# Feed-forward gate and up: the tokens' high and low parts in one 512-column matmul, with the halves added on VectorE

## The reference, cut to what matters

```python
def swiglu(u, w_in, w_out):
    a, b = jnp.split(u @ w_in, 2, axis=-1)
    return (jax.nn.silu(a) * b) @ w_out

h = h + 0.5 * swiglu(rms_norm(h, ffn1_norm), ffn1_w_in, ffn1_w_out)
...
h = h + 0.5 * swiglu(rms_norm(h, ffn2_norm), ffn2_w_in, ffn2_w_out)
```

## Time and profile before

| | before |
|---|---|
| median of 3 runs | 1435.93 us |
| profiled execution, its own time | 1435.79 us |
| its span, first to last instruction | 1434.0 us |
| PE busy | 94% of the span, 9038 matmuls |
| VectorE busy | 65% |
| ScalarE busy | 53% |
| GpSimd busy | 14% |
| mean granted TensorE clock | 0.969 |
| DMA | 263.43 MB, mean 184 GB/s |

### The profile page before, as it was taken

One profiled execution on the slowest core, in us unless ns is written; L12 is line 12 of the kernel. 1 busy time (PEld: TensorE's weight loads), 2 busy tenths in 40 slices (PEclk: granted clock), 3 DMA queues, 4 the chain that ended last, 5 costly groups with the idle time before them and its releaser, 6 DMA issues.

```text
span 1434.0 us, 22961 instructions
## 1 busy us (share of the span) xinstructions
PE 1341.9 (94%) x9038; PEld 1223.3 (85%) x9038; DVE 933.8 (65%) x1331; ACT 755.3 (53%) x1108; POOL 197.5 (14%) x163
## 2 busy tenths in 40 slices
PE   5999999979898999998989897989999999999998
PEld 5999989979698999988979787889999877787776
DVE  4655554474575555565379674584664799999996
ACT  4334345545634333355445676333653577778774
POOL 0211120021001111120020331230000000202020
PEclk9999999999999999999989899998999899999999
DMA  7666554533153665644634333324555399999991
GB/s 246 211 189 188 179 162 151 176 118 118 37 162 116 205 188 181 190 148 131 187 90 141 96 118 119 89 59 123 172 176 181 122 365 367 367 367 338 369 342 64
DMA packets 222165, 263.43 MB, mean 184 GB/s; under 512 B 14018, under 2 KB 204799, under 8 KB 221951
## 3 DMA queue, kind: packets, MB, share of 16 engines
q1 hardware_dynamic: 219520, 260.39, 56.8%
q10 hardware_dynamic: 2558, 1.86, 0.4%
HBM read 261.17 MB, written 1.05 MB: 183 GB/s over the span
## 4 chain that ended last, share of the span: by engine, by line
PE 75%; DVE 14%; ACT 6%; issue 2%; POOL 1%; DMA 1%; ACTq 0%; DVEq 0%; POOLq 0%
PE bank L526 23%; PE bank L528 22%; PE bank L527 22%; DVE sb_wlo L483 3%; DVE sb_wlo L470 3%; PE bank L621 1%; DVE sb_XC L1880 1%; PE bank L2502 1%; ACT sb_whi L464 1%; ACT sb_aw L1546 1%; DMA sb_pos<-in_positions 1%; DVE sb_st L1120 1%; PE bank L2565 1%; PE bank L2537 0%; ACT sb_sgh L1115 0%
## 5 line engine op out<-in xcount | busy, mean ns | idle before, releaser
L470 DVE TENSOR_TENSOR sb_wlo<-sb_raw,sb_whi 128x1024 fp32r<-128x1024 f32 (+4 forms) x306 | 389.4, 1316 | 224.3 <-ACT sb_whi L464 224.2
L464 ACT ACTIVATE sb_whi<-sb_raw 128x1024 fp32r<-128x1024 f32 (+4 forms) x306 | 301.4, 1037 | 238.4 <-PE bank L528 238.2
L526 PE MATMUL bank<-sb_Uh,sb_whi 128*128 128x256 f32 x1216 | 348.9, 287 | 9.2 <-DVE sb_wlo L470 5.2
L527 PE MATMUL bank<-sb_Ul,sb_whi 128*128 128x256 f32 x1216 | 346.6, 285 | 0.0
L528 PE MATMUL bank<-sb_Uh,sb_wlo 128*128 128x256 f32 x1216 | 346.4, 285 | 0.0
L526 PEld LDWEIGHTS bank<-sb_Uh,sb_whi 128*128 128x128 f32 x1216 | 236.0, 194 | 13.1 <-issue 10.1
L527 PEld LDWEIGHTS bank<-sb_Ul,sb_whi 128*128 128x128 f32 x1216 | 236.1, 194 | 0.8
L528 PEld LDWEIGHTS bank<-sb_Uh,sb_wlo 128*128 128x128 f32 x1216 | 235.9, 194 | 0.0
L526 PE MATMUL bank<-sb_whi,sb_Uh 128*128 128x256 f32 (+3 forms) x560 | 159.5, 285 | 1.1 <-DVE sb_Ul L611 0.7
L527 PE MATMUL bank<-sb_wlo,sb_Uh 128*128 128x256 f32 (+3 forms) x560 | 159.2, 284 | 0.0
L528 PE MATMUL bank<-sb_whi,sb_Ul 128*128 128x256 f32 (+3 forms) x560 | 159.1, 284 | 0.0
(11 more groups left out here) (408 smaller groups left out, 2250.3 us busy)
## 6 DMA issues: line engine op xcount, KB each, us to landing
sb_raw<-in_w_in SPq DMA_DIRECT2D x104, 512.0 KB, 4.4
sb_raw<-in_ffn_w_in SPq DMA_DIRECT2D x88, 512.0 KB, 4.5
sb_raw<-in_ffn_w_out SPq DMA_DIRECT2D x44, 512.0 KB, 3.7
sb_raw<-in_w_down SPq DMA_DIRECT2D x26, 512.0 KB, 6.9
sb_raw<-in_w_gate SPq DMA_DIRECT2D x25, 512.0 KB, 6.8
sb_raw<-in_w_up SPq DMA_DIRECT2D x25, 512.0 KB, 7.2
sb_raw<-in_w_out SPq DMA_DIRECT2D x16, 512.0 KB, 4.5
sb_raw<-in_w_ssd_branch SPq DMA_DIRECT2D x16, 512.0 KB, 4.4
```

The costliest lines, as they stand in the source:

```text
L464: nc.scalar.activation(whi[:, i % NSLOT, c], raw[:, i % NSLOT, c], ACT.Copy).then_inc(S("hi_done"), 1)
L470: nc.vector.tensor_tensor(wlo[:, i % NSLOT, c], raw[:, i % NSLOT, c], whi[:, i % NSLOT, c].bitcast(F32), ALU.subtract).then_inc(S("lo_done ...
L526: pe.matmul(o, lh, rh, start=start, stop=False, skip_group_check=True)
L527: pe.matmul(o, lh, rl, start=False, stop=False, skip_group_check=True)
```

## The change

Gate and up get two banks each, 4 and 5, 6 and 7, one per block n of 128 features. `Uh` and `Ul` become the two halves of one tensor `U`, so that for a chunk k the high and the low part of the 256 tokens can be one moving operand of two runs of 256 columns, 2048 elements (8 KB) apart. `by_feature_wide` does each triple in two matmuls: high weights with both parts, 512 columns, and low weights with the high part, 256 columns into the first half of the bank. So the first half of a bank holds high × high + low × high, the second half high × low. VectorE adds the halves of two banks in one reduction over a pair (512 sums of two). Gate's sum goes to `sgh[:, 0]`, where SiLU is taken in place, up's sum to `sgh[:, 1]`, where the product is made in place. The semaphore `ffn_sum` counts the sums; the PE's next gate or up waits for it instead of `_silu` or `_mul`. At its start `pe_ffn` claims banks 4 to 7 instead of 4 and 5. VectorE's order in the loop is: up's sum and product of chunk i, low splits of U(i+1) and D(i), gate's sum of chunk i + 1, low split of G(i+2).

```diff
-        bank = [ctx.enter_context(nc.psum_tensor(f"bank{i}", [P, 512], F32)) for i in range(8)]
+        bank = [ctx.enter_context(nc.psum_tensor(f"bank{i}", [P, 512], F32)) for i in range(4)]
+        wide_banks = ctx.enter_context(nc.psum_tensor("wide_banks", [P, 4, 512], F32))
+        bank += [wide_banks[:, i] for i in range(4)]
...
-            Uh = sb("Uh", [P, KD, T], F32R, pa)
-            Ul = sb("Ul", [P, KD, T], F32R, pa)
+            U = sb("U", [P, 2, KD, T], F32R, pa)
+        Uh, Ul = U[:, 0], U[:, 1]
...
+        def by_feature_wide(i, b):
+            wh, wl = wslab(i, KD, 256)
+            for n in range(2):
+                f, o = slice(n * P, (n + 1) * P), bank[b + n]
+                arriving = fresh.pop() if fresh else None
+                for k in range(KD):
+                    if arriving is not None:
+                        pe.wait_ge(*reach(arriving[0], k + 1))
+                    pe.matmul(o.rearrange("p (a n) -> p a n", a=2), wh[:, k, f], U[:, :, k], start=k == 0, stop=False, skip_group_check=True)
+                    last = pe.matmul(o[:, 0:T], wl[:, k, f], Uh[:, k], start=False, stop=k == KD - 1, skip_group_check=True)
+            return last
...
-            claim(4, nm + "_silu", n)
-            claim(5, nm + "_mul", n)
+            for j in range(4):
+                claim(4 + j, nm + "_sum", 2 * n - 1 + j // 2)
...
-                for j, done in enumerate(("_silu", "_mul")):
+                for j in range(2):
                     pe.wait_ge(*reach("lo_done", 2 * (g + j + 1 + off)))
                     if i is not None:
-                        pe.wait_ge(*reach(nm + done, i))
-                    by_feature(g + j, 4 + j, Uh, Ul, KD, 256).then_inc(S("slab_used"), 1)
+                        pe.wait_ge(*reach(nm + "_sum", 2 * i - 1 + j))
+                    by_feature_wide(g + j, 4 + 2 * j).then_inc(S("slab_used"), 1)
...
-            def silu(i, used_by):
-                act.wait_ge(*reach("slab_used", used_by))
-                if not (isinstance(i, int) and i == 0):
-                    act.wait_ge(*reach(nm + "_mul", i))
-                act.activation(sgh[:, 0], bank[4][:, :], ACT.Silu).then_inc(S(nm + "_silu"), 1)
+            def silu(i):
+                act.wait_ge(*reach(nm + "_sum", 2 * i + 1))
+                act.activation(sgh[:, 0], sgh[:, 0], ACT.Silu).then_inc(S(nm + "_silu"), 1)
...
+            halves_of = [wide_banks[:, 2 * j:2 * j + 2].rearrange("p c (a n) -> p c n a", a=2) for j in range(2)]
+
+            def gate_sum(i, used_by):
+                dve.wait_ge(*reach("slab_used", used_by))
+                if not (isinstance(i, int) and i == 0):
+                    dve.wait_ge(*reach(nm + "_mul", i))
+                dve.tensor_reduce(sgh[:, 0].rearrange("p (c n) -> p c n", c=2), halves_of[0], AX, ALU.add).then_inc(S(nm + "_sum"), 1)
+
             def mul(i, used_by):
                 dve.wait_ge(*reach("slab_used", used_by))
-                dve.wait_ge(*reach(nm + "_silu", i + 1))
                 if not (isinstance(i, int) and i == 0):
                     dve.wait_ge(*reach(nm + "_h", i))
-                dve.tensor_tensor(sgh[:, 1], sgh[:, 0], bank[5][:, :], ALU.mult).then_inc(S(nm + "_mul"), 1)
+                dve.tensor_reduce(sgh[:, 1].rearrange("p (c n) -> p c n", c=2), halves_of[1], AX, ALU.add).then_inc(S(nm + "_sum"), 1)
+                dve.wait_ge(*reach(nm + "_sum", 2 * i + 2))
+                dve.wait_ge(*reach(nm + "_silu", i + 1))
+                dve.tensor_tensor(sgh[:, 1], sgh[:, 0], sgh[:, 1], ALU.mult).then_inc(S(nm + "_mul"), 1)

             lo_upto(nm)
+            gate_sum(0, b + 1)
             mul(0, b + 2)
-            for k in range(3):
-                split_lo(b + 3 + k)
+            split_lo(b + 3)
+            split_lo(b + 4)
+            gate_sum(1, b + 3)
+            split_lo(b + 5)
             with dve.Fori(1, n - 1) as i:
                 mul(i, i * 3 + b + 1)
-                for k in range(3):
-                    split_lo(b + 3 + k, i)
+                split_lo(b + 3, i)
+                split_lo(b + 4, i)
+                gate_sum(i + 1, i * 3 + b + 3)
+                split_lo(b + 5, i)
```

More of the change, by code:

```diff
@@ L115, in two_blocks @@
                   [("ffn_" + k, [(nm + "_" + k, n) for nm, n in ffns]) for k in ("silu", "mul", "h", "hh")],
+                  [("ffn_sum", [("ffn1_sum", 2 * NF), ("ffn2_sum", 2 * NF)])],
                   [("ffn_x", [("ffn1_x", 4), ("ffn2_x", 4)]), ("ffn_acc", [("ffn1_acc", 3), ("ffn2_acc", 3)])],
@@ L669, in act_ffn @@
             b = slab_of[nm]
-            def silu(i, used_by):
-                act.wait_ge(*reach("slab_used", used_by))
-                if not (isinstance(i, int) and i == 0):
-                    act.wait_ge(*reach(nm + "_mul", i))
-                act.activation(sgh[:, 0], bank[4][:, :], ACT.Silu).then_inc(S(nm + "_silu"), 1)
+            def silu(i):
+                act.wait_ge(*reach(nm + "_sum", 2 * i + 1))
+                act.activation(sgh[:, 0], sgh[:, 0], ACT.Silu).then_inc(S(nm + "_silu"), 1)
             hi_upto(nm)
-            silu(0, b + 1)
+            silu(0)
             for k in range(3):
@@ L681, in act_ffn @@
             with act.Fori(1, n - 1) as i:
-                silu(i, i * 3 + b)
+                silu(i)
                 for k in range(3):
@@ L685, in act_ffn @@
             nxt["hi"] = b + 3 * n
-            silu(n - 1, b + 3 * (n - 1))
+            silu(n - 1)
             hi_upto(b + 3 * n - 1)
```

## The result

The changed kernel takes 1438.7 us (median of 20 runs, 1437.32 to 1444.07), the kernel before 1436.28 us over 20 runs beside them: the ratio is 1.0017, with a 95% interval of 1.0009 to 1.0025. It is slower by 0.17%, less than the 0.5% that the prediction called distinguishable, but the interval lies wholly above 1. The prediction had 1435.3 us, a gain of 0.6 us. The time lies inside its range; the direction was wrong.

A forecast was written before the change was run, and what follows sets the result against it. It took TensorE, busy throughout both feed-forward loops, as the bound. Matmul saving and edges, −5.4 + 0.4 + 1.6 + 0.1 + 2.7 = −0.6 us on a profiled 1435.79, gave 1435.3 us by the median; range 1430.0 to 1442.0.

The forecast's parts named there:

- the saving of the matmuls: Gate and up: a pair at 0.352 us replaces a triple at 0.360, 672 times; 5.4 us saved, between 8.9 and 0.
- edge 2: ffn2's first matmul: claiming banks 4 to 7 makes it wait for the norm's eighth low part, +1.6 us.
- Edge 1: ffn1's first slabs: gate's sum must run after the rope angles before chunk 1's gate slab starts, +0.4 us.
- Edge 3: Chunk 1's up slab in either FFN: its low part queues behind chunk 0's sum and product; +0.1 us in ffn2, 0 in ffn1.
- Edge 4: Last hidden chunk of either FFN: VectorE's split goes first and GpSimd's operation stretches, +1.36 us, twice: 2.7 us.
- a second run of the moving operand: Wide matmul: its second run of 256 columns adds some 0.005 us to 0.227, read from the experts' gate and up.
- VectorE, ScalarE and DMA in the loop: Steady loop: VectorE's two added reductions, the later SiLU and DMA slots are covered by about 11 us, costing nothing.
- Rival A: Gate and up matmuls: the fixed part goes with the runs of columns, so nothing is saved; 1440.6 us, chance 0.13.
- Its variant by the skill's 2.5 ns: Gate and up matmuls: only 2.5 ns fixed each, so 1.7 us saved; an estimated 1438.9 us, no separate chance.
- B: Gate and up: the pitch shrinks with the mix, a pair taking 0.340 us; 1427.2 us, chance 0.07.
- C: Every wide matmul: a second run 8 KB away costs far more than the experts' 4 KB; 1449.5 us, chance 0.06.
- D: Wide matmul is split again on its way, pitch as before; same time as Rival A, within its chance of 0.13.

The follow-up runs named there:

- experiment 3: The changed kernel with the token parts interleaved by chunk, so the 512 moving columns are one contiguous run: 1438.23 us, ratio 1.0009.
- experiment 6: The changed kernel with each block's eight wide matmuls first, then its eight narrow ones: 1436.28 us, ratio 0.9995.
- experiment 1: The changed kernel with each of banks 4 to 7 claimed just ahead of its first matmul: 1435.08 us, ratio 0.9989.
- experiment 2: The kernel before with the four-bank claim alone, banks 6 and 7 also claimed at each feed-forward network's start: 1442.03 us, ratio 1.0032.
- experiment 7: The changed kernel with the last chunk's hidden features made by ScalarE and VectorE instead of GpSimd: 1435.33 us, ratio 0.9983.
- experiment 8: The kernel before with its last hidden chunk made by ScalarE and VectorE, no other edit: 1436.6 us, ratio 0.9996.
- experiment 5: The changed kernel with the wide matmul taken back to two of 256 columns, sums, banks and claims kept: 1442.87 us, ratio 1.0028.

## Why the prediction was wrong

Two terms failed: the saving of the matmuls, put 1.44 us too high, and edge 2, put 1.56 us too low because its slab was priced at the full clock. Either alone would have turned the sign of a sum of −0.6; edges 1, 3 and 4 together came out 0.5 us cheaper than forecast.

**The matmuls.** Right in kind: the fixed part per matmul is real, and one in three of them saved it. The term was too large: 5.4 us against 3.96 measured (1.93 + 2.03). The pair in the loops came at 0.353 us against my 0.352, and the down slab behind it, which the prediction left at 0.227 per matmul, costs 0.03 us more a turn. A turn fell by 0.19, not 0.25. The reason I gave, a second run of the moving operand, is refuted by experiment 3. That it depends on the order of the widths is shown by experiment 6; the 0.347 of experiment 1 shows that the alternating order is not enough to bring it. By the 2.5 ns per matmul of the Trainium skill (TensorE: Matmul & The Clock Gate, Back-to-back issue gap) the saving would be an estimated 1.7 us. The measured one is over twice that.

**Edge 1.** 0.4 us expected, 0.06 measured from the start of the span. The angles ended 0.2 us earlier in that execution, and the reduction begins before they end:

```profile
31.93 0.27 DVE L1758 TENSOR_SCALAR sb_rope<-sb_rope 128x32 f32<-128x32 f32 x2
32.11 1.22 DVE L712 TENSOR_REDUCE sb_sgh<-wide_banks 128x512 f32<-128x1024 f32 x1
```

From the end of the angles to G1 it is 33.47 − 32.20 = 1.27 us, against 33.41 − 32.41 = 1.00 before. So the edge costs 0.27; the other profiled kernels with this order show 1.27 or 1.28 too.

**Edge 2.** This step failed. "Now it starts 0.14 after 446.63: +1.6 us" was right for the wait (1.83 measured), and took the first slab behind it at the full clock. It cost 1.33 us more at the lower clock, with its own saving already inside. The row to see the danger in was there. In the kernel before, with the norm's waits and transposes, 440 to 447 us had a granted clock of 0.76:

```profile
440.00:447.00 7.00, 6.29 (x35) 5.80 (x36) 4.02 (x10) 4.44 (x10) 0.65 (x2) 0.76 0.00 1
```

The change adds 1.8 us of idle PE just there. Experiments 1 and 2 show the whole of it from both sides. The Trainium skill (TensorE: Matmul & The Clock Gate, HAM oscillation — how this bites in real kernels) describes this pattern, waits (there for DMA) between groups of matmuls after which the clock is down. The 0.50 agrees. I had read the page only against the size of the saving.

**Edge 3.** 0.1 us expected, none seen in the changed kernel: U1 of ffn2 starts 5.65 us behind G1.

**Edge 4.** 1.36 us twice expected, 1.33 twice measured, by the mechanism that was named; experiments 7 and 8 confirm it.

**VectorE, ScalarE and DMA in the loop** cost nothing, as predicted; a reduction takes 1.21 to 1.23 us, against 1.22.

With the measured terms the sum is −3.96 + 0.06 + 1.83 + 1.33 + 2.66 = +1.9 instead of −0.6. The prediction's cases were all on one balance of two terms of some 5 us each; a miss of 2.5 turned the sign. Rival A gave 1440.6 without a saving, but the saving was there. Its variant by the skill's 2.5 ns, 1438.9, lies near the measured 1438.7 by luck: there a saving of 1.7 meets edges of 4.8, here 4.0 meet 5.9. That the time lies inside the range says as little, for the lower clock wasn't among the terms that set it. B, C and D did not occur.

## What to carry to other kernels

Read what a matmul costs from the distance of starts at the full clock, in each width and each order; what is saved by a wider one here is at best some 13 ns per instruction dropped, and in these loops equal widths were best kept together. When the gain per loop turn is a fraction of a microsecond, the edges decide: a claim of all banks at once, with the slow slab behind it, and a longer chain ahead of each last slab cost 5.8 us, more than the 4.0 that twenty turns gave. And price an added wait of TensorE with the slab behind it at the lower clock, not by its own length alone.

## What the runs showed of the hardware that I had not expected

- At the full clock a wide matmul costs 0.226 to 0.227 us among its like and a narrow one 0.120, but a pair in alternation 0.353 in the loops and 0.347 in some slabs ahead of them (experiments 1, 3, 6 and 7). One or two runs of moving columns make no difference (experiment 3).
- At the lower clock the fixed part is hidden: a pair takes 0.64 us for 768 columns, which are 0.64 us at 1.2 GHz, and a narrow matmul 0.21 us. The change saves nothing there.
- Behind the same wait of the PE the slab ran in part at the lower clock in five kernels of six and at the full clock in one, where the lower clock had come earlier. In experiment 5 the slab took 8.52 us instead of 5.75. In seven kernels without the wait it took at most 6.04.
